# A two-layer decoder trunk on one core: where the buffers of the SBUF plan begin

## The chip, the core and the metric

The kernel runs on one core of one Trainium2 chip. The metric is the device time of one execution in microseconds; lower is better. The kernel before took 2353.45 us, the median of three runs (2352.51 to 2356.1).

## What is computed

One sequence of 1024 tokens, model width 1024, float32 throughout. Two layers, each a token mixer and then a channel mixer (`conv_ffn`), with a residual add behind each, and a last RMSNorm.

```
layer 0: h = h + even_mixer(rms_norm(h))      # RG-LRU (512 channels) beside 8 heads of latent attention
         h = h + conv_ffn(rms_norm(h))
layer 1: h = h + odd_mixer(rms_norm(h))       # chunkwise mLSTM, 4 heads
         h = h + conv_ffn(rms_norm(h))

def conv_ffn(h, w_up, conv_w, conv_b, w_down):
    u = causal_dwconv(h @ w_up, conv_w, conv_b)     # w_up 1024 x 5632, width-3 conv over tokens
    g, val = jnp.split(u, 2, axis=-1)
    return (jax.nn.silu(g) * val) @ w_down          # w_down 2816 x 1024
```

## The kernel before

**Precision by three products.** Both operands of a large matrix product are split into a rounded part and a rest (`_hi`, `_lo`, type float32r), and each product of 128x128 weights with 512 tokens becomes three matmuls: hi x hi, hi x lo, lo x hi (`product3`, L728 to L730). The weights (the first argument of `nc.tensor.matmul`, loaded into the array) come from `whi` and `wlo`, the 512 moving columns from activations in SBUF.

**Weights.** SyncE loads tiles of 512 KB into `stage`; ScalarE or GpSimd rounds each to `whi`; GpSimd subtracts to get `wlo` (L434, L509).

**The channel mixer** (`pe_mlp`, both layers) is the longest stage. Its first three channel tiles are plain. From there the up projection runs as "up blocks" (`up_blocks`), a seven-product form of a 2x2 block product: each up block makes one gate and one value tile from seven products B11, T2, T3, T1, B21, T4, B22, in this order. A product is four k-tiles of three matmuls, so an up block is 84 matmuls. Two up blocks are followed by one down part of 96 matmuls (`down_part`, L846 to L848), whose moving operands are `hid_hi` and `hid_lo`; the loop then repeats. There are 38 up blocks in the kernel (19 in each layer).

The moving operands of the seven products are built once for each layer and then read by every up block (`operand`):

| product | moving operands, k-tile k = 0 to 3 |
|---|---|
| B11, T1, B21, B22 | `ahi`, `alo` |
| T3 | hi: pieces 0, 4, 8, 12; lo: pieces 1, 5, 9, 13 |
| T2 | hi: pieces 20 to 23; lo: pieces 3, 7, 11, 15 |
| T4 | hi: pieces 16 to 19; lo: pieces 2, 6, 10, 14 |

A piece is [128, 512] float32, 2 KB in each partition. `piece_at` puts pieces 0 to 9 at the start of the working area (`nw`), 10 to 18 behind the hidden tiles (`u1`), 19 to 24 into free halves of the weight rings.

**The memory plan.** Every SBUF buffer is placed by hand with `at(name, offset, ...)` in one arena that begins at `base`; many names share the same bytes at different times. All engines' instructions are written out in order by hand, with semaphore counts; no planner or scheduler looks at the addresses.

Of the kernel before, what the change touches and what calls it, by code (L numbers as in the profile page):

```python
# [23 lines left out]
P = 128  # L24
D = 1024
S = 1024
HALF = 512
# [95 lines left out]
def build(nc, wt, xt, pos, par, con, wqb, wkvb, wlru, wg, spill, out):  # L123
    with ExitStack() as ctx:
# [8 lines left out]
            return sems[name]  # L133


        base = -(-nc.sbuf_base // 32) * 32
        room = (nc.sbuf_usable_end - base) // 32 * 32 - 32
        ctx.enter_context(nc.sbuf_tensor("arena", [P, room // 4], F32))
        KB = 1024

        def at(name, off, shape, dt=F32):
            size = int(np.prod(shape[1:])) * 4
            assert off + size <= room, (name, off, size, room)
            return nc.alloc_sbuf_tensor_at(name, shape, dt, offset=base + off)
# [6 lines left out]
        c0 = 104 * KB  # L151
# [5 lines left out]
        c0 += 96 * 4  # L157
        cw = at("cw", c0, [P, 2, 8])
        c0 += 16 * 4
        nw = -(-c0 // 32) * 32  # L160
        sh = nw + 20 * KB
        sq = at("sq", nw, [P, 2, S])
        xnf = at("xnf", nw + 8 * KB, [P, 2, S])
# [10 lines left out]
        lc = at("lc", nw + 16 * KB, [P, S])  # L174
        ylru = at("ylru", sh + 16 * KB, [P, LRU_T, S])
        xrp = at("xrp", sh + 32 * KB, [P, S + 3])
        xc = at("xc", sh + 36 * KB + 32, [P, S])

        pbuf = at("pbuf", nw, [P, 2, S])
        ptb = at("ptb", nw + 8 * KB, [P, 2, S])  # L180
        opair = at("opair", nw + 16 * KB, [P, TT, P])
        vtok = at("vtok", sh, [P, TT, HEADS * VH])
        rt1 = at("rt1", sh + 32 * KB, [P, S])
        rt2 = at("rt2", sh + 36 * KB + 32, [P, S])
        qf = [at(f"qf{s}", sh + (34 + 4 * s) * KB + 32 * s, [P, HALF]) for s in range(2)]
        kf = at("kf", sh + 53 * KB, [P, S])
        k_hi = [at(f"k_hi{n}", off, [P, S], F32R) for n, off in enumerate((0, 16 * KB))]
        k_lo = [at(f"k_lo{n}", off, [P, S], F32R) for n, off in enumerate((4 * KB, 20 * KB))]
# [16 lines left out]

        f1 = sh + 32 * KB
        upg = at("upg", f1, [P, S + 2])
        upv = at("upv", f1 + 4 * KB + 32, [P, S + 2])
        cvg = at("cvg", f1 + 8 * KB + 64, [P, S])
        h1 = f1 + 12 * KB + 64  # L210
        hid_hi = at("hid_hi", h1, [P, 2, S], F32R)
        hid_lo = at("hid_lo", h1 + 8 * KB, [P, 2, S], F32R)
        cvv = at("cvv", h1 + 8 * KB, [P, 2, S])
# [2496 lines left out]
```

## Time and profile before

| | |
|---|---|
| median of the runs | 2353.45 us |
| the profiled execution, its own time | 2351.72 us |
| its span, first to last instruction | 2349.9 us |
| TensorE matmul busy | 2276.1 us, 97% |
| VectorE, GpSimd, ScalarE busy | 57%, 44%, 38% |
| mean granted TensorE clock | 0.991 of full speed |

The span is cut into instructions by source line. A matmul row of the timeline gives the start and a modelled duration; consecutive matmuls overlap, so what one of them costs in a dense stream is the distance from its start to the next start, not the printed duration. The starts are printed to 0.01 us, so distances are read over many matmuls.

### The profile page before, as it was taken

The numbers are of one execution on the slowest core, as the hardware profiler recorded it, in microseconds if no ns is written. First come the engines' busy times: TensorE is split into PE (matmuls) and PEld (weight loads), VectorE is DVE, ScalarE is ACT, GpSimd is POOL, SyncE is SP. The second block draws the span as 40 slices with busy tenths as digits, with TensorE's granted clock in tenths as the row PEclk, the third lists the DMA queues.
The fourth block names the chain that finished last, engine by engine and source line by source line (L and its number), as shares of the span: only waits on it lengthen the run. The fifth ranks groups of instructions, "written<-read, shape, count | busy, mean of one in ns | idle before, by whom it ended". The sixth has DMA issues, their size and how long they took to land.

```text
span 2349.9 us, 31829 instructions
## 1 busy us (share of the span) xinstructions
PE 2276.1 (97%) x10415; PEld 1850.8 (79%) x10415; DVE 1337.8 (57%) x2177; ACT 903.8 (38%) x1595; POOL 1034.3 (44%) x715
## 2 busy tenths in 40 slices
PE   6998999999999999999989999999999999999998
PEld 5786777778888888888868878878788888888886
DVE  7756565248755555555671115663875555555556
ACT  4535555124433333333441114451433333333333
POOL 3413333333555555555433332214335555555554
PEclk9999999999999999999999999999999999999998
DMA  4100000311111111111231110012111111111112
GB/s 167 45 27 1 1 0 28 117 36 45 37 54 53 47 52 46 52 54 54 64 124 55 45 45 28 27 56 92 34 36 54 54 53 47 52 46 52 54 54 90
DMA packets 34583, 122.07 MB, mean 52 GB/s; under 512 B 3840, under 2 KB 3968, under 8 KB 34240
## 3 DMA queue, kind: packets, MB, share of 16 engines
q1 hardware_dynamic: 31328, 105.39, 14.3%
q10 hardware_dynamic: 3168, 15.54, 1.7%
q8 instruction: 53, 0.87, 0.1%
q14 instruction: 34, 0.28, 0.0%
HBM read 112.52 MB, written 8.39 MB: 51 GB/s over the span
## 4 chain that ended last, share of the span: by engine, by line
PE 89%; DVE 7%; ACT 2%; issue 2%; POOL 0%; DMA 0%; ACTq 0%; DVEq 0%; POOLq 0%
PE ps L808 10%; PE ps L806 10%; PE ps L810 10%; PE ps L728 9%; PE ps L730 9%; PE ps L729 9%; PE ps L846 6%; PE ps L848 6%; PE ps L847 6%; PE ps L1571 2%; PE ps L1718 1%; PE ps L1722 1%; PE ps L1720 1%; PE ps L1559 1%; PE ps L603 1%
## 5 line engine op out<-in xcount | busy, mean ns | idle before, releaser
L509 POOL TENSOR_TENSOR wlo<-stage,whi 128x512 fp32r<-128x512 f32 x308 | 397.3, 1295 | 459.4 <-ACT whi L971 455.5
L728 PE MATMUL ps<-ahi,whi 128*128 128x512 f32 x896 | 368.8, 412 | 29.8 <-POOL wlo L434 19.1
L427 POOL TENSOR_TENSOR whi<-stage,cons 128x1024 fp32r<-128x1024 f32 x64 | 125.5, 1962 | 527.8 <-PE ps L730 313.4
L730 PE MATMUL ps<-ahi,wlo 128*128 128x512 f32 x896 | 351.2, 392 | 0.0
L729 PE MATMUL ps<-alo,whi 128*128 128x512 f32 x896 | 351.0, 392 | 0.0
L971 ACT CAST whi<-stage 128x512 fp32r<-128x512 f32 x308 | 189.2, 620 | 363.5 <-POOL stage L522 181.0
L1231 DVE TENSOR_TENSOR hT<-hT,ps 128x512 f32<-128x512 f32 x352 | 238.9, 686 | 153.9 <-PE ps L848 153.8
L846 PE MATMUL ps<-hid_hi,whi 128*128 128x512 f32 x640 | 251.3, 393 | 1.8 <-DVE hT L1231 1.6
L848 PE MATMUL ps<-hid_hi,wlo 128*128 128x512 f32 x640 | 249.8, 390 | 0.0
L847 PE MATMUL ps<-hid_lo,whi 128*128 128x512 f32 x640 | 249.6, 390 | 0.0
L806 PE MATMUL ps<-ahi,whi 128*128 128x512 f32 x608 | 236.7, 389 | 0.0
L808 PE MATMUL ps<-alo,whi 128*128 128x512 f32 x608 | 236.7, 389 | 0.0
L810 PE MATMUL ps<-ahi,wlo 128*128 128x512 f32 x608 | 236.5, 389 | 0.0
L728 PEld LDWEIGHTS ps<-ahi,whi 128*128 128x128 f32 x896 | 169.7, 189 | 71.2 <-issue 31.7
L729 PEld LDWEIGHTS ps<-alo,whi 128*128 128x128 f32 x896 | 169.7, 189 | 36.5 <-issue 2.6
L730 PEld LDWEIGHTS ps<-ahi,wlo 128*128 128x128 f32 x896 | 169.4, 189 | 36.3
L434 POOL TENSOR_TENSOR wlo<-stage,whi 128x1024 fp32r<-128x1024 f32 x68 | 171.5, 2522 | 30.3 <-ACT whi L1860 25.3
L808 PE MATMUL ps<-rpiece,whi 128*128 128x512 f32 x456 | 179.8, 394 | 0.0
L806 PE MATMUL ps<-rpiece,whi 128*128 128x512 f32 x456 | 179.3, 393 | 0.0
L810 PE MATMUL ps<-rpiece,wlo 128*128 128x512 f32 x456 | 178.1, 391 | 0.0
L846 PEld LDWEIGHTS ps<-hid_hi,whi 128*128 128x128 f32 x640 | 120.4, 188 | 30.7 <-issue 5.1
L848 PEld LDWEIGHTS ps<-hid_hi,wlo 128*128 128x128 f32 x640 | 120.5, 188 | 25.3
(323 smaller groups left out, 4089.6 us busy)
## 6 DMA issues: line engine op xcount, KB each, us to landing
stage<-in_wt SPq DMA_DIRECT2D x184, 512.0 KB, 3.6
hT<-in_xt SPq DMA_DIRECT2D x16, 256.0 KB, 9.6
hT<-in_xt ACTq DMA_DIRECT2D x8, 512.0 KB, 8.3
spill<-hT ACTq DMA_DIRECT2D x1, 4096.0 KB, 12.1
hT<-spill ACTq DMA_DIRECT2D x8, 512.0 KB, 8.2
out<-hT SPq DMA_DIRECT2D x16, 256.0 KB, 2.1
wqb_s<-in_wqb ACTq DMA_DIRECT2D x1, 1024.0 KB, 4.8
wlru_s<-in_wlru ACTq DMA_DIRECT2D x1, 512.0 KB, 6.4
```

Of the source, the lines that this page charges most:

```text
L509: nc.gpsimd.tensor_tensor(block_lo(c), src, block_hi(c).bitcast(F32), ALU.subtract).then_inc(sem(L + "b_ready"), 1)
L728: nc.tensor.matmul(bank, hi, rhs_k[0][:, tok], start=k_first, stop=False)
L729: nc.tensor.matmul(bank, hi, rhs_k[1][:, tok], start=False, stop=False)
L730: return nc.tensor.matmul(bank, lo, rhs_k[0][:, tok], start=False, stop=k_last)
L806: nc.tensor.matmul(ps[:, bank, :], block_hi(c)[:, wk], hi, start=first and k == 0, stop=False, skip_group_check=True)
L808: nc.tensor.matmul(ps[:, bank, :], block_hi(c)[:, wk], lo, start=False, stop=False, skip_group_check=True)
L810: mm = nc.tensor.matmul(ps[:, bank, :], block_lo(c)[:, wk], hi, start=False, stop=(k == 3), skip_group_check=True)
L846: nc.tensor.matmul(bank, block_hi(b)[:, wk], hid_hi[:, j, tok], start=(j == 0), stop=False)
L847: nc.tensor.matmul(bank, block_hi(b)[:, wk], hid_lo[:, j, tok], start=False, stop=False)
L848: return nc.tensor.matmul(bank, block_lo(b)[:, wk], hid_hi[:, j, tok], start=False, stop=(j == 1))
L971: nc.scalar.copy(block_hi(c), src).then_inc(b_hi, 1)
L1231: nc.vector.tensor_tensor(h, h, ps[:, bank, :], ALU.add).then_inc(sem(L + "added"), 1)
```

## The change

Six edits of the memory plan; no instruction is added, removed or reordered, and the instruction streams of all five engines are the same before and after.

```diff
-        base = -(-nc.sbuf_base // 32) * 32
+        base = -(-nc.sbuf_base // 128) * 128
...
-        nw = -(-c0 // 32) * 32
+        nw = -(-c0 // 128) * 128
         sh = nw + 20 * KB
...
-        xc = at("xc", sh + 36 * KB + 32, [P, S])
+        xc = at("xc", sh + 36 * KB + 128, [P, S])
...
-        rt2 = at("rt2", sh + 36 * KB + 32, [P, S])
-        qf = [at(f"qf{s}", sh + (34 + 4 * s) * KB + 32 * s, [P, HALF]) for s in range(2)]
+        rt2 = at("rt2", sh + 36 * KB + 128, [P, S])
+        qf = [at(f"qf{s}", sh + (34 + 4 * s) * KB + 128 * s, [P, HALF]) for s in range(2)]
...
-        upv = at("upv", f1 + 4 * KB + 32, [P, S + 2])
-        cvg = at("cvg", f1 + 8 * KB + 64, [P, S])
-        h1 = f1 + 12 * KB + 64
+        upv = at("upv", f1 + 4 * KB + 64, [P, S + 2])
+        cvg = at("cvg", f1 + 8 * KB + 128, [P, S])
+        h1 = f1 + 12 * KB + 128
```

`nc.sbuf_base` is 16481 in this program, so `base` is 16512 = 129 x 128 by either rule: the first edit moves nothing. `c0` behind the small tables is 111552 bytes past `base`, so `nw` goes from 111552 to 111616. Where the buffers begin, as byte addresses modulo 128 and 256:

| buffers | mod 128 before -> after | mod 256 before -> after |
|---|---|---|
| `stage`, `whi`, `wlo`, `ahi`, `alo`, `cons`, pieces 19 to 24, `k_hi`, `k_lo`, `q_hi1`, `q_lo1` | 0, not moved | 128, not moved |
| `pars` | 32, not moved | 160, not moved |
| pieces 0 to 9, `hT`, `sq`, `acc`, `diag`, `pbuf`, `ptb`, `opair`, `vtok`, `ylru`, `lat`, `lat_hi`, `lat_lo`, `kf`, `qf0`, `q_hi0`, `q_lo0`, `wh_hi`, `wh_lo`, `wghi`, `wglo`, `upg`, the buffers of the mLSTM | 64 -> 0 | 64 -> 128 |
| `xc`, `rt2`, `qf1` | 96 -> 0 | 96 -> 0 |
| `upv` | 96 -> 64 | 96 -> 192 |
| `cvg`, `hid_hi`, `hid_lo`, pieces 10 to 18, `sqf`, `accf`, `diagf` | 0 -> 0 (moved by 128 bytes) | 128 -> 0 |

So `pars` and `upv` do not begin at a multiple of 128 after the change either.

## Rows read from the trace of the kernel before

**Rows 1.** The page: busy time, and the chain that ended last by line
```profile
PE 2276.1 (97%) x10415; PEld 1850.8 (79%) x10415; DVE 1337.8 (57%) x2177; ACT 903.8 (38%) x1595; POOL 1034.3 (44%) x715
...
PE ps L808 10%; PE ps L806 10%; PE ps L810 10%; PE ps L728 9%; PE ps L730 9%; PE ps L729 9%; PE ps L846 6%; PE ps L848 6%; PE ps L847 6%; PE ps L1571 2%; PE ps L1718 1%; PE ps L1722 1%; PE ps L1720 1%; PE ps L1559 1%; PE ps L603 1%
```

**Rows 2.** Busy time by stretch: layer 0's channel mixer, layer 1's, the attention
```profile
60.00:480.00 420.00, 394.77 (x2092) 313.61 (x2092) 229.83 (x399) 188.79 (x366) 146.66 (x98) 0.98 0.09 32
...
560.00:1060.00 500.00, 500.00 (x2193) 411.05 (x2192) 303.54 (x452) 198.03 (x328) 266.40 (x205) 1.00 0.16 49
...
1700.00:2330.00 630.00, 629.84 (x2763) 517.15 (x2762) 379.84 (x566) 249.31 (x411) 336.75 (x260) 1.00 0.16 49
```

**Rows 3.** TensorE's timeline, one down part, two up blocks (start, duration)
```profile
646.22 0.39 PE L846 MATMUL ps<-hid_hi,whi 128*128 128x512 f32 x1
...
667.98 0.39 PE L806 MATMUL ps<-ahi,whi 128*128 128x512 f32 x1
...
687.19 0.39 PE L806 MATMUL ps<-ahi,whi 128*128 128x512 f32 x1
...
689.91 0.39 PE L806 MATMUL ps<-rpiece,whi 128*128 128x512 f32 x1
...
692.68 0.39 PE L806 MATMUL ps<-rpiece,whi 128*128 128x512 f32 x1
...
694.78 0.39 PE L806 MATMUL ps<-rpiece,whi 128*128 128x512 f32 x1
...
695.47 0.40 PE L806 MATMUL ps<-ahi,whi 128*128 128x512 f32 x1
...
698.20 0.39 PE L806 MATMUL ps<-ahi,whi 128*128 128x512 f32 x1
...
700.92 0.39 PE L806 MATMUL ps<-rpiece,whi 128*128 128x512 f32 x1
...
703.69 0.39 PE L806 MATMUL ps<-ahi,whi 128*128 128x512 f32 x1
...
706.41 0.40 PE L846 MATMUL ps<-hid_hi,whi 128*128 128x512 f32 x1
```

**Rows 4.** Instructions that read the pieces (ns min/median/max, first and last start)
```profile
L806 PE MATMUL ps<-rpiece,whi x456: 388/394/398, 610.5 to 2302.2; 128*128 128x512 f32 x152
L808 PE MATMUL ps<-rpiece,whi x456: 392/394/398, 610.7 to 2302.4; 128*128 128x512 f32 x152
L810 PE MATMUL ps<-rpiece,wlo x456: 388/389/394, 611.0 to 2302.7; 128*128 128x512 f32 x152
```

**Rows 5.** TensorE's timeline, the gate product of layer 1: its ends
```profile
1226.88 0.39 PE L1654 MATMUL ps<-ahi,wghi 128*128 128x512 f32 x1
...
1237.87 0.39 PE L728 MATMUL ps<-ahi,whi 128*128 128x512 f32 x1
```

**Rows 6.** Groups by line and shape, the other engines
```profile
L509 POOL TENSOR_TENSOR wlo<-stage,whi 128x512 fp32r<-128x512 f32 x308 | 397.3, 1295 | 459.4 <-ACT whi L971 455.5 <-POOL wlo L509 3.9
...
L1231 DVE TENSOR_TENSOR hT<-hT,ps 128x512 f32<-128x512 f32 x352 | 238.9, 686 | 153.9 <-PE ps L848 153.8
...
L1162 DVE TENSOR_TENSOR hid_lo<-ps,hid_hi 128x512 fp32r<-128x512 f32 x88 | 58.3, 684 | 0.3
...
L628 ACT ACTIVATE sq<-hT 128x512 f32<-128x512 f32 x48 | 29.4, 627 | 28.3 <-DVE acc L673 10.1 <-DVE hT L1231 9.4 <-POOL acc L417 6.5
...
L461 POOL TENSOR_TENSOR q_lo<-qf,q_hi 96x512 fp32r<-96x512 f32 x16 | 20.8, 1300 | 3.7 <-ACT q_hi L1975 2.6
...
L628 ACT ACTIVATE sqf<-hT 128x512 f32<-128x512 f32 x32 | 20.1, 632 | 133.9 <-DVE hT L1404 63.2 <-DVE hT L1384 50.2 <-DVE accf L673 20.4
...
L1864 ACT ACTIVATE ahi<-hT,pars 128x512 fp32r<-128x512 f32 x16 | 11.4, 712 | 1.8 <-DMA hT<-in_xt 1.8
```

**Rows 7.** VectorE's timeline before the down part of Rows 3
```profile
700.88 1.28 DVE L1162 TENSOR_TENSOR hid_lo<-ps,hid_hi 128x512 fp32r<-128x512 f32 x2
```

## The prediction

> **What bounds the kernel.** I read the page first: TensorE is busy for 97% of the span, and the chain that ended last runs through its matmul lines almost alone, the three lines of the up blocks (L806, L808, L810) with 10% each, the three of the down parts with 6% each [rows 1]. Then the stretches: in the two channel mixers TensorE is busy for all of 500 us and for 629.84 of 630, while VectorE (303.54 us), GpSimd (266.40) and ScalarE (198.03) leave much of the 500 free; the clock column is 1.00 there, so it stays at the upper of its two levels, 2.4 GHz [rows 2]. In such a stretch the time is the number of matmuls times the distance between their starts. A change of addresses can only act by making that distance shorter or longer, so the third view is the timeline of starts, product by product [rows 3].
>
> **What the starts show.** The down part from 646.22 to 667.98 takes 21.76 us for 96 matmuls, 226.7 ns each; the product B11 from 687.19 to 689.91 takes 2.72 us for 12, the same [rows 3]. Their moving operands all begin at a multiple of 128 bytes. T3 starts at 692.68, and its fourth k-tile at 694.78: nine matmuls in 2.10 us, 233 ns each [rows 3]. These nine read pieces 0, 1, 4, 5, 8 and 9, which begin 64 bytes past a multiple of 128. So a moving operand 64 bytes off costs about 6.7 ns more by these rows (2.10 us less 9 x 226.7 ns, shared by nine). T2 takes 2.77 us (689.91 to 692.68) and T4 2.77 us (700.92 to 703.69), 50 ns over B11 each, although only two of their twelve matmuls read a piece that is off by 64 (pieces 3 and 7, or 2 and 6) [rows 3]. Their even beat seems to be upset by such a read and to need some matmuls to settle; T1, which reads `ahi` and `alo` alone, comes right behind T3 and takes 2.73. The printed durations say the same more coarsely: medians of 394, 394 and 389 ns over 456 each for the pieces [rows 4].
>
> T2 and T4 fetch their hi parts from quite different places (the ring of the weights, and the area behind the hidden tiles), and still take the same 2.77 us. What they share is the lo pieces off by 64. That speaks for the start address and against the region of SBUF. A second witness lies elsewhere: the gate product of layer 1 has aligned moving operands and weights (`wghi`, `wglo`) that are off by 64. It takes 10.99 us for 48 matmuls, 229.0 ns each, 2.3 above the aligned beat [rows 5].
>
> **The sum.** *Up blocks.* The two from 667.98 to 706.41 take 38.43 us; 168 matmuls at 226.7 ns (21.76 us x 168/96) would take 38.08 us. The excess is 0.35 us for two, and there are 38 (rows 4: 456 matmuls of L806 on pieces, 12 to an up block, four in each of three products). 19 x 0.35 = 6.6 us, all on the path. After the change pieces 0 to 9 begin at a multiple of 128, as every other operand of the up blocks does, so I expect the whole excess to go: **-6.6 us**. The printed hundredths leave it uncertain by 19 x 0.01 to 0.02, some 0.3 us.
>
> *Gate product.* 48 x 2.3 ns = **-0.1 us**.
>
> *Attention and mLSTM.* Operands there move from 64 to 0 too (`lat_hi`, `q_hi0`, `vtok`, the mLSTM's). But in 60 to 480 us TensorE idles 25 of 420 us and changes instruction shape all the time [rows 2], so the beat never settles. Bounds: nothing, or 6.7 ns for each of the 2092 matmuls, 14 us less; most of these are plain tiles of `ahi` and `alo` that are aligned already. I take 0, being nearest to the stretch's idle time, and keep -1 us as a practical end.
>
> *VectorE, ScalarE, GpSimd.* The trace holds pairs of the same work at either alignment: `hT` (off by 64) plus PSUM 686 ns against `hid_lo` (aligned) 684; squares from `sq` (off) 627 against `sqf` (aligned) 632; GpSimd's rest from `qf` (off by 64 or 96) 1300 for 512 elements against 1295 from `stage` (aligned) [rows 6]. No alignment effect above 5 ns and no common sign: 0. Even a gain would be off the path.
>
> *DMA.* Loads into `hT` now begin 64 bytes later. The only wait that names them ahead of TensorE's first tiles is 1.8 us in total [rows 6]. Bounds: all of it gone, or doubled; I take 0.
>
> *Does the gain reach the end?* TensorE shortens a pair of up blocks by 0.35 us, so what it needs next must be ready that much earlier. The last `hid_lo` is finished at 700.88 + 1.28 = 702.16 and first read at 706.41 [rows 7, 3]: 4.2 us of cover. GpSimd's blocks have the larger cover, idle 234 of 500 us [rows 2]. Nothing takes the wait's place. If that cover were gone, the price would be at most the 6.6 us themselves.
>
> Sum: -6.7, taken as -6.6 because the gate product is within the reading error. From the profiled execution's own 2351.72 us this gives 2345.1. It lies 1.7 us under the median of the runs, so for a median I take 2353.45 - 6.6 = **2346.9 us**, 0.28% faster.
>
> **Rival 1: the start address does nothing.** The beat of 233 ns may belong to something that T2, T3 and T4 have in common beside alignment, such as changing between distant buffers from one matmul to the next. The time would stay at 2353.5. For it: in T2, ten of twelve matmuls read aligned pieces and the product is still 50 ns long [rows 3]. Against it: in T3 the beat is 233 exactly as long as the operands are off, and the gate product shows an excess with `ahi` and `alo` as its moving operands [rows 5].
> The Trainium skill leads to this rival: "SBUF — State Buffer", Specifications (TRN2), gives cachelines of 16 bytes in a partition. By it a 2 KB row touches 128 lines whether it begins at 64 or at 0, and the change would be worth nothing; the same page says of its rule on operand starts (Operand start alignment) that it is about legality and not speed. The 233 against 226.7 ns stands against the reading that 16 bytes are all that matter; the measurement decides.
>
> **Rival 2, slower: the fast phase is 128 modulo 256, not 0 modulo 128.** All the fast 512-column operands of the trace, and the weights beside them, begin at 128 modulo 256, and none begins at 0. The change puts `hid_hi`, `hid_lo` and pieces 10 to 18 at 0 modulo 256. If that phase is as slow as 64 is, 2112 matmuls on the hidden tiles (640 x 3 in the down parts and 64 x 3 in the first ones) cost 6.3 to 6.7 ns more, some 13.5 us, and in an up block 13 matmuls become slow (lo parts of T2 and T4 for k = 2, 3; hi parts of T4 for k = 0 to 2, six matmuls; T3's k = 3, three) in exchange for the 13 that become fast: no gain there. 2353.5 + 13.5 = 2367. It decides from the point where a hidden matmul costs 6.6 us / 2112 = 3.1 ns more. Against it: it needs a preference for an odd phase, for which no row speaks.
>
> **Rival 3, more gain.** The reverse: starts at 0 modulo 256 are better still, because part of the 226.7 ns is the same loss at half strength. 2112 x 6.5 ns = 13.7 us on top of 6.6: 2333. Against it: 64 modulo 256 is then a quarter off and should not be worse than 128.
>
> **That the change doesn't do what it says** holds for `base`, `pars` and `upv`; none of them is an operand of TensorE, so it costs the forecast nothing.
>
> **How the numbers follow.** Forecast 66%, rival 1 (with half effects) 22%, rival 2 6%, rival 3 4%, others 2%. About 0.2%, 4.7 us, is what a measurement of this kernel can tell from no change, so faster means under 2348.7. The forecast's own range is 2345 to 2349; it falls over the bound in one case of ten. Faster: 0.59 + 0.04 + 0.03 = 0.66. Same: 0.07 + 0.20 = 0.27. Slower: 0.07. The range must take in rival 1 up to 2355, since leaving it out would leave out more than two in ten; it leaves out rivals 2 and 3 and the edges: 2344 to 2355.
>
> **What will show it.** T2, T3 and T4 each take 2.72 us in the timeline of starts, two up blocks 38.08 us, and the medians for the pieces fall from 394 to 389 ns. The gate product takes 10.88 us. The down part stays at 21.76: if it takes 22.4, rival 2 holds; if it takes 21.1, rival 3. If T3's first nine still take 2.10 us, rival 1 holds. The forecast is also wrong if the up blocks shorten and TensorE shows new waits for GpSimd or VectorE in the channel mixers.

## The result, and the profile after

The changed kernel takes 2366.37 us (median, 2365.43 to 2368.37) against 2354.77 for the kernel before in the same comparison: ratio 1.0054, 95% interval 1.0042 to 1.0065. It is slower by about 12 us. The prediction was wrong, in sign and in size; the time is that of rival 2.

The page after, in the lines that answer to [rows 1] and to the groups of the down part and of the pieces (busy us, mean ns of one):

```profile
PE 2288.4 (97%) x10415; PEld 1852.6 (78%) x10415; DVE 1338.8 (57%) x2177; ACT 904.1 (38%) x1595; POOL 1034.6 (44%) x715
...
L846 PE MATMUL ps<-hid_hi,whi 128*128 128x512 f32 x640 | 254.8, 398 | 1.7 <-DVE hT L1231 1.4
L848 PE MATMUL ps<-hid_hi,wlo 128*128 128x512 f32 x640 | 252.9, 395 | 0.0
L847 PE MATMUL ps<-hid_lo,whi 128*128 128x512 f32 x640 | 252.8, 395 | 0.0
...
L808 PE MATMUL ps<-rpiece,whi 128*128 128x512 f32 x456 | 178.4, 391 | 0.0
```

TensorE is busy for 12.3 us more (2288.4 less 2276.1); the other engines stand where they were. The three lines of the down part print 5 ns more a matmul than in the kernel before, the pieces up to 3 ns less (medians of 390, where 394 became 389 in the forecast).

TensorE's timeline of starts after the change: one down part, and the products of an up block from B11 to T1 and from T4 to B22 (it answers to [rows 3]):

```profile
708.08 0.49 PE L846 MATMUL ps<-hid_hi,whi 128*128 128x512 f32 x1
...
730.48 0.40 PE L806 MATMUL ps<-ahi,whi 128*128 128x512 f32 x1
...
733.25 0.39 PE L806 MATMUL ps<-rpiece,whi 128*128 128x512 f32 x1
...
735.98 0.39 PE L806 MATMUL ps<-rpiece,whi 128*128 128x512 f32 x1
...
738.71 0.39 PE L806 MATMUL ps<-ahi,whi 128*128 128x512 f32 x1
...
741.46 0.39 PE L806 MATMUL ps<-ahi,whi 128*128 128x512 f32 x1
...
744.18 0.40 PE L806 MATMUL ps<-rpiece,whi 128*128 128x512 f32 x1
...
746.94 0.40 PE L806 MATMUL ps<-ahi,whi 128*128 128x512 f32 x1
```

The down part takes 22.40 us instead of 21.76: 233.3 ns a matmul, a break of some 0.1 us at its start included (the first matmul prints 0.49). The distance from one start to the next, called the beat below, was 233 ns before too, in nine of T3's matmuls. T2 (733.25 to 735.98) and T3 (to 738.71) take 2.73 us each instead of 2.77 and 2.79, so they did gain; T4 still takes 2.76, since eight of its twelve matmuls read pieces 16 to 18, 10 or 14, which moved to 0 modulo 256. The gain in T2 and T3 is real and is buried under 20 down parts that lose 0.64 us each by these rows, 0.60 on average over the two traces (22.41 against 21.81), some 12 us.

The gate product answers to [rows 5]; its weights now begin where the activations do, modulo 256:

```profile
1234.20 0.39 PE L1654 MATMUL ps<-ahi,wghi 128*128 128x512 f32 x1
...
1245.08 0.39 PE L728 MATMUL ps<-ahi,whi 128*128 128x512 f32 x1
```

10.88 us for 48 matmuls, the aligned beat of 226.7 ns, as forecast.

### The profile page after: what moved, and what is told of

Same layout as the page of the kernel before. It is cut to its first block, busy times and chain, and to the rows that moved or that the text cites. A ratio compares the mean times of both kernels' runs of the same rounds, so it can differ in the third digit from the quotient of the medians.

```text
span 2364.0 us, 31829 instructions
## 1 busy us (share of the span) xinstructions
PE 2288.4 (97%) x10415; PEld 1852.6 (78%) x10415; DVE 1338.8 (57%) x2177; ACT 904.1 (38%) x1595; POOL 1034.6 (44%) x715
## 4 chain that ended last, share of the span: by engine, by line
PE 88%; DVE 7%; ACT 3%; issue 2%; POOL 0%; DMA 0%; ACTq 0%; DVEq 0%; POOLq 0%
PE ps L806 10%; PE ps L808 10%; PE ps L810 10%; PE ps L728 8%; PE ps L730 8%; PE ps L729 8%; PE ps L846 6%; PE ps L847 6%; PE ps L848 6%; PE ps L1571 2%; PE ps L1718 1%; PE ps L1722 1%; PE ps L1720 1%; PE ps L1559 1%; PE ps L603 1%
## 5 line engine op out<-in xcount | busy, mean ns | idle before, releaser
L846 PE MATMUL ps<-hid_hi,whi 128*128 128x512 f32 x640 | 254.8, 398 | 1.7 <-DVE hT L1231 1.4
L848 PE MATMUL ps<-hid_hi,wlo 128*128 128x512 f32 x640 | 252.9, 395 | 0.0
L847 PE MATMUL ps<-hid_lo,whi 128*128 128x512 f32 x640 | 252.8, 395 | 0.0
L846 PEld LDWEIGHTS ps<-hid_hi,whi 128*128 128x128 f32 x640 | 120.4, 188 | 35.6 <-issue 7.0
L848 PEld LDWEIGHTS ps<-hid_hi,wlo 128*128 128x128 f32 x640 | 120.4, 188 | 28.5
```

Source lines behind the costliest of these rows:

```text
L846: nc.tensor.matmul(bank, block_hi(b)[:, wk], hid_hi[:, j, tok], start=(j == 0), stop=False)
L847: nc.tensor.matmul(bank, block_hi(b)[:, wk], hid_lo[:, j, tok], start=False, stop=False)
L848: return nc.tensor.matmul(bank, block_lo(b)[:, wk], hid_hi[:, j, tok], start=False, stop=(j == 1))
```

## The experiments

The question after the result: is 128 modulo 256 a good address by itself (theory B), or does only the distance between the moving operand and the weights count (theory A)? In both kernels so far the weights of the channel mixers begin at 128 modulo 256, so their down parts and up blocks can't tell the two apart. Only the gate product of the kernel before spoke for theory A: its weights alone were off, its moving operands at 128, and it had the longer beat [rows 5]. "Distance" below is the start of the moving operand less that of the weights, modulo 256.

**best_phase**: the changed kernel with every operand of the channel mixers at distance 0.

```diff
-        h1 = f1 + 12 * KB + 128
+        h1 = f1 + 12 * KB + 256
```

> The changed kernel with the hidden tiles and everything behind them 128 bytes further, so that every operand of the channel mixers begins at 128 modulo 256, where the weights begin. Phase theory (a moving operand is slow unless it begins at 128 modulo 256, or at the phase of the weights): down part back to 21.76 us, two up blocks 38.08 us, time 2354.8 - 6.7 = 2348 us, ratio 0.997. Rival (the loss of the changed kernel has to do with something else that moved, such as hT or the small buffers): down part stays at 22.4 us and the time at 2366.

2351.94 us against 2354.52, ratio 0.9992 (0.9983 to 1.0001): it takes back the whole loss of 14 us but gives little more, and the interval does not exclude that it gives nothing. The beat is as expected: the down part, with 0.1 us more between its first two starts behind a wait, takes 21.91 us, and the products of the up blocks are back at 2.72 us each.

```profile
708.42 0.39 PE L810 MATMUL ps<-ahi,wlo 128*128 128x512 f32 x1
708.89 0.49 PE L846 MATMUL ps<-hid_hi,whi 128*128 128x512 f32 x1
...
730.80 0.39 PE L806 MATMUL ps<-ahi,whi 128*128 128x512 f32 x1
```


**hidden_only**: the kernel before with the hidden tiles alone at distance 128.

```diff
-        h1 = f1 + 12 * KB + 64
+        h1 = f1 + 12 * KB + 192
...
-        u1 = h1 + 16 * KB
+        u1 = h1 + 16 * KB + 128
```

> The kernel before with hid_hi and hid_lo alone 128 bytes further (0 modulo 256); pieces 10 to 18 are kept at 128 modulo 256 and pieces 0 to 9 at 64. Phase theory: down part 22.4 us, two up blocks as before 38.43 us, time 2354.8 + 13.5 = 2368 us (ratio 1.0057). Rival (the region behind nw as a whole is to blame): time as before.

2367.65 us, ratio 1.0058 (1.0043 to 1.0074). The down part takes 22.31 us:

```profile
709.35 0.39 PE L846 MATMUL ps<-hid_hi,whi 128*128 128x512 f32 x1
...
731.66 0.39 PE L806 MATMUL ps<-ahi,whi 128*128 128x512 f32 x1
```

Two tiles moved by 128 bytes make the whole loss of the change.

**arena_128**: the kernel before, everything 128 bytes further.

```diff
-        base = -(-nc.sbuf_base // 32) * 32
+        base = -(-nc.sbuf_base // 32) * 32 + 128
```

> The kernel before with the whole arena 128 bytes further: weights, activations and hidden tiles all at 0 modulo 256, pieces 0 to 9 at 192. Theory A, the phase counts against the weights that are loaded at the same time: no distance between two buffers has changed, down part 21.76 us, two up blocks 38.43 us, time 2354.8 (ratio 1.000). Theory B, the address itself must be 128 modulo 256: about 8000 matmuls of 512 columns lose 6.5 ns each, time 2354.8 + 52 = 2407 us.

2354.53 us, ratio 1.0001 (0.9991 to 1.001). The down part:

```profile
704.84 0.39 PE L846 MATMUL ps<-hid_hi,whi 128*128 128x512 f32 x1
...
726.60 0.39 PE L806 MATMUL ps<-ahi,whi 128*128 128x512 f32 x1
```

21.76 us with `hid_hi` at 0 modulo 256, where it costs 22.40 in the changed kernel. Theory B falls: 128 modulo 256 is not good by itself, nor 0 bad.

**weights_128**: best_phase with `whi` and `wlo` alone 128 bytes further (buffers behind them make room, their distance to each other unchanged modulo 256; some attention buffers that share these bytes move by 128 too).

```diff
-        whi = at("whi", 8 * KB, [P, RING, 1024], F32R)
-        wlo = at("wlo", 24 * KB, [P, RING, 1024], F32R)
-        ahi = at("ahi", 40 * KB, [P, KT, S], F32R)
+        whi = at("whi", 8 * KB + 128, [P, RING, 1024], F32R)
+        wlo = at("wlo", 24 * KB + 128, [P, RING, 1024], F32R)
+        ahi = at("ahi", 40 * KB + 256, [P, KT, S], F32R)
...
```

> The best-phase kernel with whi and wlo alone 128 bytes further (0 modulo 256), all moving operands at 128 modulo 256. Theory A (phase against the weights): every matmul on ahi, alo, pieces and hidden tiles loses 6 to 7 ns, time 2348 + 8000 x 6.5 ns = 2400 us. Theory B (address of the moving operand): no change, 2348 us. Theory C (both operands must begin at 128 modulo 256, each for itself): weights off cost 2 to 3 ns each as in the gate product, 2348 + 8000 x 2.3 ns = 2366 us.

2389.74 us, ratio 1.0157 (1.0142 to 1.0173), 38 us above best_phase.

```profile
712.51 0.40 PE L846 MATMUL ps<-hid_hi,whi 128*128 128x512 f32 x1
...
734.91 0.40 PE L806 MATMUL ps<-ahi,whi 128*128 128x512 f32 x1
```

22.40 us again in 19 of the 20 complete down parts (22.46 in the other), and 39.20 us for two up blocks, with not one moving operand of the channel mixers moved against another modulo 256. So the distance to the weights is what counts: theory A. It costs 38 us where 52 were charged for 8000 matmuls. The channel mixers pay in full, and the stretch ahead of them hardly at all: their first down part starts at 589.31 us, in best_phase at 588.92. The plain tiles there slow down too (227.0 to 232.3 ns a matmul between 110 and 160 us), so part of the loss must be hidden, perhaps behind TensorE's waits; no run shows where.

**phase_64_192, phase_32_96, phase_160_224**: best_phase with the hidden tiles at another distance in each layer (layer 0, layer 1), the pieces behind them 256 bytes further.

```diff
-        hid_hi = at("hid_hi", h1, [P, 2, S], F32R)
-        hid_lo = at("hid_lo", h1 + 8 * KB, [P, 2, S], F32R)
+        shift = {"F0": 64, "F1": 192}
+        hid_his = {L: at("hid_hi" + L, h1 + d, [P, 2, S], F32R) for L, d in shift.items()}
+        hid_los = {L: at("hid_lo" + L, h1 + d + 8 * KB, [P, 2, S], F32R) for L, d in shift.items()}
...
-        u1 = h1 + 16 * KB
+        u1 = h1 + 16 * KB + 256
```

> The best-phase kernel, the hidden tiles 64 bytes past the weights' phase in layer 0 and 192 past it in layer 1; everything else at the weights' phase (moving start minus weights' start, modulo 256). Phase theory with the sign counting: layer 0 as the gate product of the kernel before (distance +64), down part 229 ns a matmul, 22.0 us; layer 1 as pieces 0 to 9 of the kernel before (distance -64), 233.4 ns, 22.4 us. Rival, only being off counts: both 22.4 us.

> The same with 32 (layer 0) and 96 (layer 1). If the loss grows with the distance: layer 0 about 228 ns a matmul (21.9 us), layer 1 about 231 ns (22.2 us). If being off at all counts: both 233.4 ns, 22.4 us.

> The same with 160 (layer 0) and 224 (layer 1). If the loss falls off toward 256: 160 as 128, 233.4 ns and 22.4 us; 224 less, about 230 ns and 22.1 us. If being off at all counts: both 22.4 us.

One down part of each layer in phase_64_192, from its first matmul to the first of the next up block (the line numbers are two higher in these kernels):

```profile
707.97 0.50 PE L848 MATMUL ps<-hid_hiF,whi 128*128 128x512 f32 x1
...
730.06 0.39 PE L808 MATMUL ps<-ahi,whi 128*128 128x512 f32 x1
...
1848.91 0.50 PE L848 MATMUL ps<-hid_hiF,whi 128*128 128x512 f32 x1
...
1871.41 0.39 PE L808 MATMUL ps<-ahi,whi 128*128 128x512 f32 x1
```

22.09 us at distance 64, 22.50 at 192. The same two starts in the other kernels give the table; a down part that follows a wait holds some 0.1 us more, as the 21.91 of best_phase (distance 0) does and the 22.41 at 96 does not. The second row is free of that: the mean beat from the ninth matmul on, as the median over the down parts. The down part at 128 is the changed kernel's, the beat that of weights_128.

| distance | 0 | 32 | 64 | 96 | 128 | 160 | 192 | 224 |
|---|---|---|---|---|---|---|---|---|
| down part, us | 21.91 | 22.49 | 22.09 | 22.41 | 22.40 | 22.59 | 22.50 | 22.50 |
| beat, ns | 226.7 | 233.3 | 228.9 | 233.3 | 233.4 | 234.3 | 233.3 | 233.4 |

In each of these six layers the ten complete down parts are alike to 0.11 us. Of the expectations for 64 and 192 the one with the sign holds (64 costs a third of the loss, as in the gate product, where the distance is 64 too). For the rest "being off at all counts" is right, and a loss that grows with distance is not: 32 bytes cost as much as 128. Single runs: 2363.58, 2363.74 and 2366.89 us, against 2352.78.

**hidden_split**: only `hid_lo` off by 128 in layer 0, only `hid_hi` off (by -128) in layer 1. One run.

```diff
...
+        shift = {"F0": (0, 128), "F1": (-128, 0)}
...
```

> The best-phase kernel with one hidden tile off by 128 in each layer: hid_lo alone in layer 0 (one matmul of three), hid_hi alone in layer 1 (two of three). If each matmul pays for its own moving operand: layer 0 6.7/3 = 2.2 ns on average, 22.0 us a down part; layer 1 4.5 ns, 22.2 us. If an upset beat costs as much as a whole slow run: both about 22.3 us.

```profile
648.82 0.40 PE L848 MATMUL ps<-hid_hiF,whi 128*128 128x512 f32 x1
...
671.01 0.40 PE L808 MATMUL ps<-ahi,whi 128*128 128x512 f32 x1
...
709.25 0.49 PE L848 MATMUL ps<-hid_hiF,whi 128*128 128x512 f32 x1
...
731.74 0.40 PE L808 MATMUL ps<-ahi,whi 128*128 128x512 f32 x1
...
1849.25 0.39 PE L848 MATMUL ps<-hid_hiF,whi 128*128 128x512 f32 x1
...
1871.25 0.40 PE L808 MATMUL ps<-ahi,whi 128*128 128x512 f32 x1
```

2359.30 us. The down part at 709.25 takes 22.49 us and the one at 1849.25 22.00: here the one operand of three that is off costs 0.6 us, the two of three 0.2, the reverse of the expected order. But layer 0 is not of one kind, though all its down parts read the same addresses: the one at 648.82 takes 22.19. Of its ten complete ones the first takes 21.97, three take 22.19 to 22.28 (a beat of 231.1 ns) and six 22.49 or 22.50 (233.3). In layer 1 all ten take 21.98 to 22.10 (228.9). So a matmul does not simply pay for its own moving operand, and with only some operands off the distances alone do not fix the beat. The two halves also differ in the layer and in the sign of the shift: +128 and -128 are the same modulo 256 but not modulo 512, the step from one 128x128 block of weights to the next. The changed kernel shows a milder form of it: ten of its complete down parts have a beat of 232.3 to 232.5 ns, ten of 233.4. What picks the value stays open.

**wlo_128**: weights_128 with `whi` left in place, everything else as there. One run.

> The best-phase kernel with wlo alone 128 bytes further. whi is the weights of the first two matmuls of each three, wlo of the third, and the load of a matmul's weights runs beside the matmul before it. If the moving read clashes with the load running beside it, one matmul in three is slow, the average is 226.7 + 2.2 = 229 ns at least and the time between 2352 and 2390, near 2366 us. If it were only a matter of the moving operand's own start, nothing changes: 2352 us.

```profile
714.98 0.39 PE L846 MATMUL ps<-hid_hi,whi 128*128 128x512 f32 x1
...
737.16 0.39 PE L806 MATMUL ps<-ahi,whi 128*128 128x512 f32 x1
```

22.18 us for 96, 231.0 ns each: two thirds of the full loss where one third was expected. The time, 2380.92 us, is inside the stated bounds and 15 us over the value named. The starts say which matmuls pay. Over its down parts the mean from a start to the next is 226.8 ns for L846 (`hid_hi` with `whi`), 232.5 for L847 (`hid_lo` with `whi`), beside which the block of `wlo` is loaded, and 234.1 for L848, which uses it. So two matmuls in three are slow for one operand in three, the one beside which the shifted weights are loaded and the one that uses them. Why the second pays is not shown, and hidden_split does not follow from this.

**no_difference_before, no_difference_best**: where the missing 4 us of best_phase went. GpSimd's subtraction a12 - a11 is left out, so the result of these two kernels is wrong.

```diff
-                nc.gpsimd.tensor_tensor(a12, a12, a11, ALU.subtract).then_inc(sem(L + "b_sum"), 1)
+                pool.sem_inc(sem(L + "b_sum"), 1)
```

> The kernel before without GpSimd's last subtraction of each up block (a12 - a11, 1.29 us, 38 times): part of the computation is left out, so that the load of the next stage tile and the blocks of the down part come earlier. TensorE waits only 1.5 us at the starts of the down parts in the kernel before; expected 2353.5, ratio 0.9995, and 2354.5 if these waits have another cause.

> The best-phase kernel without the same subtraction. Theory: of the 6.4 us that TensorE's shorter beat gives, 2 us came back as a wait of the down part's first matmul for GpSimd's wlo (its chain is a fixed latency: rest, stage slot free, load, cast, rest). With the chain 1.3 us shorter the waits go, and the time is 2354.5 - 6.4 - 1.5 = 2346.6 us, ratio 0.9966, 6 us under the run without the subtraction in the old plan. Rival: the wait is no chain of GpSimd; then the gain stays at 2 us, ratio 0.999.

In the old plan 2352.92 us against 2353.36, ratio 1.0001 (0.9992 to 1.001); in the new one 2345.81, ratio 0.9970 (0.9960 to 0.9980). Leaving it out is worth nothing where TensorE has the longer beat and 5 us where it has the shorter one (0.9992 to 0.9970). From the first to the last complete down part of each layer the two channel mixers take 1077.12 us together in no_difference_best and 1080.69 in best_phase, 1083.36 in no_difference_before and 1084.85 before: waits, and the breaks that they leave, cost 3.6 us with the shorter beat and 1.5 with the longer, so 2.1 us of the gain came back there. The rest of the missing 4 us is not located. Two profiled executions can differ by that much in a stretch that the subtraction doesn't touch: the first down part starts at 588.92 us in best_phase and at 586.31 in no_difference_best. The chain shows in best_phase: ScalarE's timeline before the down part at 708.89,

```profile
706.76 1.14 ACT L971 CAST whi<-stage 128x512 fp32r<-128x512 f32 x2 [2.17 <-DMA stage<-in_wt]
```

GpSimd's,

```profile
704.18 1.29 POOL L509 TENSOR_TENSOR wlo<-stage,whi 128x512 fp32r<-128x512 f32 x1 [1.24 <-ACT whi L971]
707.46 2.54 POOL L509 TENSOR_TENSOR wlo<-stage,whi 128x512 fp32r<-128x512 f32 x2 [1.99 <-ACT whi L971]
```

and TensorE's at 1843 us, where the gap is widest:

```profile
1842.53 0.39 PE L810 MATMUL ps<-ahi,wlo 128*128 128x512 f32 x1
1843.61 0.49 PE L846 MATMUL ps<-hid_hi,whi 128*128 128x512 f32 x1 [0.69 <-POOL wlo L509]
```

The first of the two blocks at 707.46 is done at 708.7, and the down part starts at 708.89: TensorE takes it as it comes. In the kernel before, GpSimd's timeline has the same block end at 706.15, 0.26 us ahead of the down part at 706.41 [rows 3]:

```profile
704.88 2.54 POOL L509 TENSOR_TENSOR wlo<-stage,whi 128x512 fp32r<-128x512 f32 x2 [2.00 <-ACT whi L971]
```

ScalarE's cast that feeds it waits for the load, which waits for the stage slot that GpSimd frees one block after the subtraction.

**best_early**: best_phase, nothing left out, the subtraction one block earlier.

```diff
                 block_rest(L, q + 4, c + 4, a12)
+                pool.wait_ge(sem(L + "b_ready"), q + 5)
+                nc.gpsimd.tensor_tensor(a12, a12, a11, ALU.subtract).then_inc(sem(L + "b_sum"), 1)
                 block_rest(L, q + 5, c + 5, a22)
                 pool.wait_ge(sem(L + "b_ready"), q + 6)
                 pool.sem_inc(stage_free[sv], 1)
-                nc.gpsimd.tensor_tensor(a12, a12, a11, ALU.subtract).then_inc(sem(L + "b_sum"), 1)
```

> The best-phase kernel with nothing left out, but GpSimd's subtraction a12 - a11 moved ahead of the rest of block q + 5 (it needs only block q + 4 done). ScalarE's cast of block q + 6 then no longer waits for it (1.67 us in the kernel before), the stage slot is free earlier and the blocks of the down part too. Theory (the 2 us lost are this chain): no gap at the starts of the down parts, 2346 us, ratio 0.9970, as the run without the subtraction. Rival (GpSimd's order matters elsewhere, for instance the cast of block q + 5 or the first stage slot comes later by 1.3 us): gaps stay, 2350 to 2352 us.

2346.52 us against 2353.44, ratio 0.9964 (0.9950 to 0.9977): 7 us faster than the kernel before by the medians and 8.5 by the ratio, and some 20 faster than the changed one. GpSimd and TensorE at the same place (line numbers one higher from here on):

```profile
703.68 2.54 POOL L509 TENSOR_TENSOR wlo<-stage,whi 128x512 fp32r<-128x512 f32 x2 [1.01 <-ACT whi L972]
```

```profile
706.17 0.39 PE L847 MATMUL ps<-hid_hi,whi 128*128 128x512 f32 x1
...
727.93 0.39 PE L807 MATMUL ps<-ahi,whi 128*128 128x512 f32 x1
```

The block is there at 704.95, 1.2 us ahead, and the down part takes 21.76, as all twenty complete ones do; two up blocks take 38.08 each time.

## Why the prediction was wrong

- **Where to look: right.** In the channel mixers TensorE's beat is the time, and the change acted there, and hardly elsewhere (the gate product, 0.1 us).
- **The step that failed: "After the change pieces 0 to 9 begin at a multiple of 128, as every other operand of the up blocks does, so I expect the whole excess to go", and with it the down parts at an unchanged 21.76 us.** I read the rows of before as "off by 64 is slow, a multiple of 128 is fast", and so charged nothing for operands that went from one multiple of 128 to another. The gate product, which I took as a second witness for the address, has its weights off and so bears as well on the distance. The runs show that what counts is the distance to the weights modulo 256 (arena_128: everything moved, nothing lost; weights_128: weights moved, all lost). `hid_hi`, `hid_lo` and pieces 10 to 18 went from distance 0 to 128. That is +12 us in the down parts (20 x 0.60, the mean over the trace) and +1.3 in the first ones (one in each layer, 22.39 instead of 21.76), and in the up blocks pieces 10 to 18 took back nearly all that pieces 0 to 9 gave: two of them take 38.36 us (730.48 to the down part at 768.84) instead of 38.43, but the 18 pairs between complete down parts take 691.9 us together instead of 692.2, waits included. With the gate product it is some 13 us, where the medians differ by 11.6 and the profiled executions by 14.1. The table of the change held every address for this.
- **The -6.6 us of the up blocks**: T2 and T3 fell to 2.73, not 2.72, and T4 stayed at 2.76. With all operands at distance 0 the excess does go entirely (best_phase, best_early), so the size was right for a plan that this change is not. In this change the term measured -0.3.
- **The gate product, -0.1 us**: right, 10.99 to 10.88.
- **VectorE, ScalarE, GpSimd, DMA: 0**: busy times moved by 1 us or less.
- **The cover of 4.2 us**: wrong. I checked `hid_lo` and set GpSimd aside by its idle share. Its block was ready 0.26 us before it was needed, and in best_phase 2.1 us of the gain came back as such waits. An engine that idles 47% can still be just in time, as here, where its work hangs on a load that waits for a slot it frees itself. In the changed kernel this was not what decided; it would have cost the forecast a third of its gain.
- **Rival 1** (nothing): wrong. **Rival 2** (0 modulo 256 is slow): its price, 2367, and its place, a down part of 22.4 us, were right; its reason, a preferred address, is not, as arena_128 shows. I gave it 6%, since "it needs a preference for an odd phase, for which no row speaks"; a preference for the phase of the weights would not have been odd. That its number came out is in part luck: a loss by distance has the same price in this plan as a loss by address. **Rival 3**: wrong.
- The Trainium skill ("SBUF — State Buffer", Specifications (TRN2)) has 16-byte cachelines; a start that moves by 32 bytes keeps to them and costs 0.58 us in 96 matmuls (22.49 against 21.91). They do not explain this loss.

## What to carry to other kernels

In a dense stream of 512-column float32r matmuls, put the moving operands and the weights at the same start modulo 256 bytes; rounding every buffer to 128 does not do that and can undo it. Before moving a buffer for alignment, list each operand's start against that of the operand read beside it, before and after, by a larger modulus than the one in question. When a bound engine gets a shorter beat, measure the cover of each of its producers by their finish times, not by their idle share. All this is from one kernel, at one shape and type; other shapes and types were not run.

## What the runs showed of the hardware

- The start of a 512-column matmul follows the one before by 226.7 ns when moving operand and weights are in phase modulo 256, and by 233.3 to 234.3 ns at every other distance tried but 64 (233.4 in weights_128, 22.40 us for 96): about 3%. A distance of 256 is as good as 0: best_phase has the hidden tiles 256 bytes further from the weights than the kernel before, modulo 1024, and both show 226.7 ns.
- A matmul can pay for weights that are loaded beside it: with `wlo` alone off (wlo_128), 232.5 ns for the matmul that uses `whi` while `wlo` is loaded, 234.1 for the one that uses `wlo`, 226.8 for the third.
- The same addresses can give more than one beat: 231.1 and 233.3 ns in layer 0 of hidden_split.
- The first two starts of a down part behind a wait are some 330 ns apart, not 227 (best_phase at 708.89): each such break costs 0.1 us beside the wait itself.
- The loss is nearly all there at a distance of 32 bytes and a third of it at 64; the cause of that exception, and of what hidden_split shows, stays open. I read the effect as a clash of the moving read with the load of the weights beside it; no run shows the clash itself.
